# Nine short convolutions issued beside the first two delta-rule tiles instead of ahead of them, with one row buffer in another tile

## What is computed

```
xn = rmsnorm(hp, norm1);  qa, ka, va, qkv_b, z, b, a = split(xn @ w_in)
oa = differential attention of qa, ka, va            # and of a paged cache
conv = silu(sum(conv_w[j] * xpad[:, j:j + t] for j in range(4)))
q, k, v = split(conv);  q = l2norm(q) * 128**-0.5;  k = l2norm(k)
ob, state = gated delta rule(q, k, v, decay, beta)   # in chunks of 64
hp = hp + merge(oa, ob, z) @ w_out
hp = hp + peer(rmsnorm(hp, norm2))                   # 128 experts of 16384 for each token
```

## Time and profile before

| | |
|---|---|
| times of three runs | 2055.47, 2058.57, 2064.84 us |
| profiled execution | 2057.25 us, its span 2055.5 us |
| PE busy | 1692.7 us, 82% of the span |
| DVE, ACT, POOL busy | 65%, 39%, 37% |
| DMA queues | q0 73.0%, q1 17.2% of 16 engines' span |
| bytes moved | 763.10 MB, mean 371 GB/s |
| chain that ended last | DMA 34%, PE 34%, DVE 16%, ACT 7% |
| costliest line | PE L2228, 942.7 us busy |

### The profile page before, as it was taken

The page is one execution under the profiler, slowest core; times in us unless marked ns, Lnnn a source line. Parts: engine busy times, 40 slices in busy tenths (PEclk is TensorE's granted clock), DMA queues, the critical chain, the costliest instruction groups (busy, mean ns, idle before and its releaser), DMA issues.

```text
span 2055.5 us, 20563 instructions
## 1 busy us (share of the span) xinstructions
PE 1692.7 (82%) x6211; PEld 852.5 (41%) x6211; DVE 1337.1 (65%) x3023; ACT 801.8 (39%) x2371; POOL 763.6 (37%) x670
## 2 busy tenths in 40 slices
PE   7698899988897878889787888979796677866777
PEld 2243464547453445445344535534452223532111
DVE  1344514344897657887665888874698866779554
ACT  1342322132545523563543446363344323333432
POOL 2111110111444444435344353634434544554442
PEclk9899999999999999999899999999899889997999
DMA  9999723226999999999999999999999999999997
GB/s 339 357 313 387 243 90 118 92 103 258 405 411 410 426 428 428 426 426 415 427 423 426 427 426 398 418 426 415 427 426 412 427 427 426 427 427 427 427 427 311
DMA packets 137591, 763.10 MB, mean 371 GB/s; under 512 B 15327, under 2 KB 24559, under 8 KB 60536
## 3 DMA queue, kind: packets, MB, share of 16 engines
q0 software_dynamic: 88448, 622.22, 73.0%
q1 hardware_dynamic: 45552, 132.26, 17.2%
q10 hardware_dynamic: 3480, 7.31, 1.0%
HBM read 745.75 MB, written 16.26 MB: 371 GB/s over the span
## 4 chain that ended last, share of the span: by engine, by line
DMA 34%; PE 34%; DVE 16%; ACT 7%; issue 4%; POOL 2%; SPq 1%; ACTq 0%; DVEq 0%; POOLq 0%
DMA sb_uv<-in_peer_uv,sb_eidx 31%; PE bank L2228 14%; PE bank L1836 7%; DVE sb_uv L1815 7%; PE bank L2195 2%; PE bank L2157 2%; POOL sb_uv L1020 2%; DVE sb_hres L1789 1%; ACT sb_diag L1394 1%; ACT L1383 1%; PE bank L1950 1%; DMA sb_xin<-pre_conv 1%; ACT sb_ew L1387 1%; PE bank L1962 1%; DMA sb_hres<-pre_conv 1%
## 5 line engine op out<-in xcount | busy, mean ns | idle before, releaser
L2228 PE MATMUL bank<-sb_uv,sb_diag 128*128 128x512 f32 (+1 forms) x1860 | 942.7, 642 | 284.3 <-ACT sb_diag L1394 273.5
L1020 POOL DMA_INDIRECT sb_uv<-in_peer_uv,sb_eidx x576 | 682.7, 1185 | 861.2 <-PE bank L2228 663.3
L1815 DVE CUSTOM_DVE_ANT_0 sb_uv<-sb_uv,sb_xn 128x1024 f32<-128x1024 f32 x576 | 699.7, 1221 | 293.8 <-DMA sb_uv<-in_peer_uv,sb_eidx 291.2
L2228 PEld LDWEIGHTS bank<-sb_uv,sb_diag 128*128 128x128 f32 (+1 forms) x1860 | 331.5, 193 | 772.9 <-ACT sb_diag L1394 451.7
L1383 ACT ACTIVATE sb_gel<-sb_h 128x1 f32<-128x1 f32 x576 | 116.3, 202 | 761.5 <-DVE sb_h L1815 758.6
L1836 PE MATMUL bank<-sb_w,sb_xnT 128*128 128x512 f32 (+1 forms) x560 | 266.7, 619 | 21.4 <-DMA sb_w<-in_w_sections 8.5
L1394 ACT ACTIVATE sb_diag<-sb_stay,sb_ew 128x128 f32<-128x128 f32 (+1 forms) x465 | 183.2, 394 | 46.0 <-PE bank L2228 2.5
L1387 ACT ACTIVATE sb_ew<-sb_gel,sb_gate 128x1 f32<-128x1 f32 x576 | 169.7, 295 | 19.8
L1836 PEld LDWEIGHTS bank<-sb_w,sb_xnT 128*128 128x128 f32 (+1 forms) x560 | 98.7, 187 | 144.2 <-issue 120.4
L1789 DVE SCALAR_TENSOR_TENSOR sb_hres<-sb_uv,sb_ew,sb_hres 128x1024 f32<-128x1024 f32 x111 | 142.3, 1282 | 0.1
L2195 PEld LDWEIGHTS bank<-sb_rT,sb_zone 128*128 128x128 f32 x832 | 101.0, 196 | 16.0 <-issue 15.5
(11 more groups left out here) (345 smaller groups left out, 1596.5 us busy)
## 6 DMA issues: line engine op xcount, KB each, us to landing
sb_zone<-in_w_route SPq DMA_DIRECT2D x11, 2304.0 KB, 11.9
sb_w<-in_w_sections SPq DMA_DIRECT2D x40, 512.0 KB, 6.9
sb_zone<-in_w_mixer SPq DMA_DIRECT2D x8, 2048.0 KB, 15.8
sb_uv<-in_peer_uv,sb_eidx POOLq DMA_INDIRECT x576, 14.4
sb_sS<-in_cache_kT SPq DMA_DIRECT2D x32, 256.0 KB, 8.2
sb_zone<-in_cache_kT SPq DMA_DIRECT2D x32, 256.0 KB, 7.4
sb_held<-in_cache_v SPq DMA_DIRECT2D x32, 256.0 KB, 8.2
sb_zone<-in_cache_v SPq DMA_DIRECT2D x32, 256.0 KB, 6.2
```

Of the source, the lines that this page charges most:

```text
L1020: nc.gpsimd.indirect_dma_start(uv[:, m % RING, :], None, i["peer_uv"], bass.IndirectOffsetOnAxis(ap=eidx[:, t % 2, n:n + 1], axis=0)).then ...
L1815: nc.vector.tensor_tensor_reduce(out=uv[:, m % RING, 0:D], in0=uv[:, m % RING, 0:D], in1=xn2[:, t % 2, :], scale=1.0, scalar=0.0, op0=ALU. ...
L2228: ins = nc.tensor.matmul(bank[half][0:rows, :], lhsT=G["diag"][:, d % DIAGS, 0:rows], rhs=uv[:, m % RING, D + 512 * half:D + 512 * half + ...
```

## The change

`conv_at` now depends on the tile. A list `CONVS` puts the convolutions in a new order: those of the first two tiles of each section keep the place behind their unit (they are now `m` = 0 to 5), and the nine of the other three tiles (`m` = 6 to 14: q, k, v, three tiles each) get nominal times 225, 245, ... 385, beside `gdn(0)` (208 on) and `gdn(1)` (302 to about 386). Because the sections now come twice, the taps are loaded six times in place of three. The second row buffer is no longer `hres` but the first 2048 columns of `resident`, a tile that later holds routing weights; their load waits for all convolutions and moves from nominal 330 to 402. The wait of `gdn(0)` on ACT for all 15 silus goes, as `hres` is no longer shared. Semaphore counts follow the new order.

```diff
+CONVS = [(sec, n) for sec in range(3) for n in range(2)] + [(sec, n) for sec in range(3) for n in range(2, NT)]
...
 def conv_at(m):
-    return after(C0 + m, 13)
+    sec, n = CONVS[m]
+    return after(C0 + NT * sec + n, 13) if n < 2 else early_at(225 + 20 * (m - 6))
...
-        cv = [x.rearrange("p a (j n) -> p (a j) n", j=2) for x in (F["xin"][:, :, :], hres[:, :, :])]
+        cv = [F["xin"][:, :, :].rearrange("p a (j n) -> p (a j) n", j=2), resident[:, 0:2 * D].rearrange("p (j n) -> p j n", j=CONV_W)]
...
+        def taps_loads(m):
+
+            return sum(k == 0 or CONVS[k][0] != CONVS[k - 1][0] for k in range(m + 1))
+
+        def normed_before(m):
+
+            return sum(CONVS[k][0] < 2 for k in range(m))
...
                 def resident_loads():
-                    yield after(V0 + PT, 3)
+                    yield early_at(402)
+                    sp.wait_ge(s_cs, 3 * NT)
                     sp.wait_ge(s_vst, 16 * (NT + 1))
...
                 def conv_inputs():
-                    for m in range(3 * NT):
-                        sec, n = divmod(m, NT)
-                        t = ORDER[n]
+                    for m, (sec, n) in enumerate(CONVS):
+                        t, raw = ORDER[n], NT * sec + n
...
                         yield conv_at(m) - 9
-                        if n == 0:
+                        if m == 0 or CONVS[m - 1][0] != sec:
                             if m:
                                 pool.wait_ge(s_conv, 3 * (m - 1) + 1)
                             pool.dma_start(cw, i["conv_w"][0:1, :, ch].broadcast_to([128, CONV_W, HW])).then_inc(s_cw, 16)
...
                             for half in range(2):
                                 act.wait_ge(s_sT, 2 * h + half + 1)
-                                if h == 0:
-                                    act.wait_ge(s_cs, 3 * NT)
```

More of the change, by code:

```diff
@@ L495, in conv_loads @@
         def conv_loads(m):
-            return sum((1 if k % NT else 1 + CONV_W) for k in range(m + 1) if conv_buffer[k] == conv_buffer[m])
+            return sum((1 if CONVS[k][1] else 1 + CONV_W) for k in range(m + 1) if conv_buffer[k] == conv_buffer[m])
+        def taps_loads(m):
+            return sum(k == 0 or CONVS[k][0] != CONVS[k - 1][0] for k in range(m + 1))
+        def normed_before(m):
+            return sum(CONVS[k][0] < 2 for k in range(m))
         def conv_before(m):
@@ L507, in spill_count @@
         def spill_count(m):
-            return sum(k % NT > 0 for k in range(m % 3, m + 1, 3))
+            return sum(CONVS[k][1] > 0 for k in range(m % 3, m + 1, 3))
         def kst_count(u):
@@ L1463, in conv @@
                 def conv(m):
[L1464 removed]
+                    (sec, n), j = CONVS[m], normed_before(m)
                     rows = ROWS[ORDER[n]]
```

73 lines of the change are left out of this document (36 added, 37 removed).

## The result

Seven runs of each kernel on one chip: 2061.59 us before (2055.47 to 2065.39), **2074.86 us after** (2070.11 to 2077.81). The ratio is 1.0062, its 95% interval 1.0043 to 1.0081. The change makes the kernel 13.3 us slower, against a forecast of 4 us faster. The profiled execution after took 2072.24 us, its span 2070.4: 14.9 more than the span before.

A forecast was written before the change was run, and what follows sets the result against it. From 515 us the sweep is DMA-bound with fixed bytes, so only its start matters; gains 12.0 less losses 8.0 give -4.0 us, 2053.3 from the profiled 2057.25, stated as a 2054.5 median, range 2044 to 2067.

The forecast's parts named there:

- The kind of sweep: From 515 us on, a DMA-bound stream of fixed bytes; its start moves the end microsecond for microsecond, its length unchanged.
- Term A: PE's weights wait at 189.58: SP reaches the load 1.6 us earlier, it lands 2.7 faster; gain 4.3 us.
- Rival 1: Weights at 189.58 land no faster, page loads alone filling the engines; gain there 1.6, time 2057 us; chance 0.19.
- Term B: PE's stall at 217.23 for L1674 goes, and the slow product with it; gain 4.7 us.
- Term C: PE's stall for `kb` at 249.73 goes; gain 2.95 us, ends 2 and 4.5.
- The losses: Nine convolutions beside `gdn(0)` and `gdn(1)` delay PE at five places, 8.0 us in sum, ends 3 and 14.
- the multiplies of 13 and 14: At `dl` and the output of `gdn(1)`, partly hidden in DVE's wait for POOL; losses there 1.1 and 2.0 us.
- The term of convolution 11: Adds and scaling, 1.9 us each, precede the subtraction of 369.59 in `gdn(1)`, cover 2.6; loss 1.2 us.
- rival 3: Delta rule's chain in front: late convolutions 9 to 14 each cost their DVE work, no cover holding; 2077 us; chance 0.08.
- The term of 12: Its silu on ACT delays a unit's copy PE already awaits at 386.64; loss 1.8 us, between 0 and 4.2.
- The marks: Wrong if no weights wait near 185 us, lead under 6 at 260, or waits 260 to 455 up over 14.
- Rival 4: POOL's work and the multiplies block each other at all nine, 1.44 us each, 13.0 more; 2067.6 us; chance 0.05.

The follow-up runs named there:

- e1: Changed kernel with its late convolutions due 16 apart instead of 20: 2084.11 us, ratio 1.0108.
- e2: Changed kernel with POOL asking for rows and taps of the late convolutions 7 sooner: 2074.94 us, against 2074.86.
- e8: Changed kernel with all nine late convolutions at new places off updates, `dl` and barrier, rows asked for 7 sooner: 2054.15 us, ratio 0.9966.
- e12: e8 with four loads of weights moved on SP between the halves of the fourth pair's keys: 2047.89 us, ratio 0.9926.
- e14: e8 with the tenth convolution alone put back from 267 to 285, among the sample updates: 2059.96 us, ratio 0.9996.
- e5: Changed kernel with the fifteenth convolution 10 sooner and the fourteenth moved from 365 to 353, off `dl`: 2063.36 us, ratio 1.0003.
- e4: Changed kernel with only six convolutions late, 20 apart from 225 to 325: 2059.28 us, ratio 0.9991.
- e6: e4 with the fourth to sixth late convolutions due at 302, 322, 342, none among the sample updates: 2061.23 us, ratio 1.0000.
- e9: e8 with the fourteenth convolution put back from 350 to 364, ahead of `dl`, and the fifteenth from 375 to 376: 2054.88 us, ratio 0.9965.
- e11: Changed kernel with all convolutions in their old places, keeping the new row buffer and later routing weights: 2061.63 us, ratio 1.0000.
- e13: Kernel before with only the four loads of weights moved on SP, as in e12: 2060.33 us, ratio 1.0000.

## Why the prediction was wrong

**The kind of sweep.** Right that it is bound by transfers and that its start moves its end, and wrong that its length stays. It was 4.7 us longer in the execution profiled after the change. PE met a spell of half clock there from 620 to 635 us, in the delta rule of tile 2, and the DMA share fell to 0.72, which is 4.2 us of idle transfers in 15. Five of the other kernels (e1, e2, e8, e12, e14) show the same spell, with 3 to 5 us of idle transfers around it, the others about 1 or none. The sweep also grew without it (by 4.3 us in e5), and in e12 by 11.0. What decides it was not tested.

**Term A, failed** (4.3 forecast, 0.9 measured, by the offset at 199.60). The step that failed is "SP comes to it earlier by the stores that have left its queue": SP's page loads took up what the stores had freed. The landing gained 0.65 us and not 2.7. Rival 1 had the landing right; it too counted 1.6 for SP. That SP's order, not the transfers, sets this time was right (e12), and so was the forecast that the wait would exceed 6.64.

**Term B**: 4.7 forecast, 3.3 measured (-0.9 to -4.2, the slow products behind the fold gone with most of its wait, of which 1.32 us stayed). **Term C**: 2.95 forecast, with an upper end of 4.5; 4.9 measured (-4.2 to -9.1), since the slow work behind the wait went too.

**The losses**, by place:

| convolutions | forecast | measured |
|---|---|---|
| 6, 7, 8 | 0 | 0 |
| 9, sample updates | 1.9 | 3.6 (5.2 to 5.3 in e2, e4, e5, e14) |
| 10, 11, 12, levels | 3.0 | 3.6 |
| 13, `dl` | 1.1 | 6.0 |
| 14, barrier | 2.0 | 6.1 |
| sum | 8.0 | 19.3 |

The places were right, and most of the mechanisms; the sizes were not, in the main for one reason: **the price of a wait was taken to be the wait.** Of the 11.3 us by which the sum was short, 2.1 are longer waits (they grew by 10.1, not 8.0) and 9.2 are work that ran slower. The step that failed stands in the part on what comes in its place: a cover that is 1 or 2 us short was priced at 1 or 2 us. The first part of the prediction had read off the rows that "Behind a stall the same work also runs slower for a while" and had used it for the gains (B), but not for one of the losses. At `dl` the wait was 2.70 us and PE lost 6.0. TensorE ran at a granted clock of 0.50 from 410 to 415 us behind it. The Trainium skill (TensorE: Matmul & The Clock Gate, "HAM oscillation — how this bites in real kernels") says that a wait for data can send the engine back to its lower clock, so that the work behind it starts slow, and that this is paid at every such wait. By that rule, the trace agrees at `dl` and at the barrier. It does not everywhere: the Trainium skill speaks there of longer waits than the 2.70 us here, PE ran at full clock behind 2.75 us in e6, and at half clock from 313 us on with no wait ahead of it in e8.

Two terms of the sum failed by a step of their own: the multiplies of 13 and 14 were said to fill DVE's wait for POOL (some 2 us at `dl`, 1.1 at the output of `gdn(1)`), and POOL's power was held up beside them, to 3.63 and 2.99 us. At `dl` this is the difference between the wait forecast, 1.1, and the 2.70 measured, as e9 shows by taking the multiply away (0.71).

The term of convolution 11 counted adds and the scaling step, with rows on time. Its multiply waited 7.85 us for rows, and PE waited at the level behind it (360.70), which rival 3 had named, as well as at the one behind the scaling (370.37); with rows asked for sooner the levels lost 0.6 us and not 3.6 (e2). The term of 12 was 1.8, and PE's wait for ACT grew by 0.5.

At the barrier the forecast was 3.3 us less 1.3 that PE gets back at 434.44; the rows give 4.5 (4.2 to 8.7), then 2.9 more for products at half clock (6.18 us for eight at 437.84), less 1.3. Of the 4.1 us by which it was missed, 2.9 are the clock and 1.2 the chain: POOL's power held the output back by 0.8 more than forecast, and the store, behind a silu that ended at 433.9, landed at 436.6, 0.4 later than counted.

**The marks** that the prediction set for itself did not fire: PE was 9.1 us ahead at 260 us (under 6 would have told), and waited for weights near 185 us. Its waits from 260 to 455 us grew by some 10 us, not by over 14. A sum of waits misses what is slow behind them; the offset of like instructions does not.

**Rivals.** 3 had the price right (2077, measured 2074.86) and half of the cause: the covers did fail at 9, 11, 13 and 14, but by waits of 0.4 to 5.6 us with slow work behind them, not by DVE's 4.2 us at each of six. That its sum came so close is luck. It had 0.08. Rival 4 (POOL and DVE in each other's way, 0.05) was right at two places, and they were two that mattered: no multiply of a late convolution took over 2.29 us in the changed kernel, but POOL's powers beside those of 13 and 14 took 2 us more each. Its price of 1.44 at all nine did not come out. The buffer alone was rightly put at 0 (e11), and so, by the same run, were the later routing weights.

## What to carry to other kernels

Lay the instructions of the engine that never changes order beside each other and read the differences of their starts: each gain and loss then has a place. Where TensorE is nearly full, a wait of 2 to 3 us can cost up to two and a half times its length (3.2 us lost for 2.75 in e6, 3.6 to 5.3 for 2.4, 6.0 to 7.1 for 2.7); give it a range and not its length. Do not count DVE work as hidden in a wait for POOL if it runs beside POOL's own instruction. And move work off the few tight places before asking whether there is too much of it. A relief may be worth nothing until the next limit behind it is gone too: the same move on SP gave nothing in e13 and 6.3 us in e12.
